# Decoder layer on one core: mixer weights split during the input projection, merge by chunks of 512 tokens

## The reference, cut to what matters

```
proj = h @ w_in                                  # (2048 x 1024) @ (1024 x 4864)
u, q, k, v, gate_pool, gate_att = split(proj)
pooled = einsum(multiscale_pool(u), w_pool_group)        # 512 channels
y_pool = (pooled * pool_scale) @ w_branch_pool           # 512 -> 1024
o = sum over 3 groups of softmax(lse) * group_output     # 256 channels
y_att = o @ w_branch_att                                 # 256 -> 1024
merged = sigmoid(gate_pool) * y_pool + sigmoid(gate_att) * y_att
y = merged @ w_out
x = x + gate * rmsnorm(y);  then a routed expert layer on x
```

## Time and profile before

| | |
|---|---|
| median of 3 runs | 2729.76 us (2728.51 to 2739.48) |
| the profiled execution: its time, its span | 2733.67 us, 2731.9 us |
| busy, share of the span | PE 87%, PEld 75%, DVE 49%, ACT 34%, POOL 20% |
| mean granted PE clock | 0.946 of full speed |
| merge | 1219 to 1415 us |
| mix_out, up to the start of its loop over tiles | 1415 to 1460 us |

### The profile page before, as it was taken

The page is one execution under the profiler, slowest core; times in us unless marked ns, Lnnn a source line. Parts: engine busy times, 40 slices in busy tenths (PEclk is TensorE's granted clock), DMA queues, the critical chain, the costliest instruction groups (busy, mean ns, idle before and its releaser), DMA issues. The chain is left out here.

```text
span 2731.9 us, 39222 instructions
## 1 busy us (share of the span) xinstructions
PE 2381.6 (87%) x13485; PEld 2039.5 (75%) x13486; DVE 1338.9 (49%) x1673; ACT 933.1 (34%) x1541; POOL 549.2 (20%) x375
## 2 busy tenths in 40 slices
PE   3599999999999968876969995699999999999990
PEld 3488888888888857764857884588898988988880
DVE  7552111123232257636534445888666384655536
ACT  3200000000000035533322221587666375655533
POOL 2311111111111020002334552222222222212220
PEclk9999999999999989957989996799999999999995
DMA  6123222223424233226555444599999597878847
GB/s 231 46 77 123 90 95 98 86 104 111 138 92 138 107 122 119 92 98 216 212 185 195 155 155 153 186 353 356 320 305 284 137 353 231 282 217 279 246 146 292
DMA packets 291435, 493.43 MB, mean 181 GB/s; under 512 B 21145, under 2 KB 226481, under 8 KB 281778
## 3 DMA queue, kind: packets, MB, share of 16 engines
q1 hardware_dynamic: 272658, 424.53, 44.9%
q0 software_dynamic: 14112, 51.39, 8.0%
q10 hardware_dynamic: 4608, 16.78, 1.5%
HBM read 374.98 MB, written 117.64 MB: 180 GB/s over the span
## 5 line engine op out<-in xcount | busy, mean ns | idle before, releaser
L357 PE MATMUL proj_psum<-h_hi,proj_w_hi 128*128 128x512 f32 x1216 | 481.7, 396 | 19.0 <-POOL proj_w_lo L342 19.0
L359 PE MATMUL proj_psum<-h_hi,proj_w_lo 128*128 128x512 f32 x1216 | 481.4, 396 | 0.0
L358 PE MATMUL proj_psum<-h_lo,proj_w_hi 128*128 128x512 f32 x1216 | 481.4, 396 | 0.0
L1585 PE MATMUL moe_p_gu<-moe_hi_gu,moe_xT_hi 128*128 128x256 f32 x1536 | 437.4, 285 | 1.7 <-DVE moe_xT_lo L1694 1.7
L378 DVE COPY proj_out<-proj_psum 128x512 f32<-128x512 f32 x152 | 123.7, 815 | 634.4 <-PE proj_psum L359 633.3
L1586 PE MATMUL moe_p_gu<-moe_lo_gu,moe_xT_hi 128*128 128x256 f32 x1536 | 428.7, 279 | 0.0
L1587 PE MATMUL moe_p_gu<-moe_hi_gu,moe_xT_lo 128*128 128x256 f32 x1536 | 428.6, 279 | 0.0
L1513 DVE TENSOR_TENSOR moe_lo_gu<-raw_gu,moe_hi_gu 128x1024 fp32r<-128x1024 f32 x256 | 302.1, 1220 | 23.5 <-ACT moe_hi_gu L1507 19.4
L335 ACT ACTIVATE proj_w_hi<-proj_raw 128x1024 fp32r<-128x1024 f32 x38 | 40.4, 1062 | 781.5 <-PE proj_psum L359 748.0
L1586 PEld LDWEIGHTS moe_p_gu<-moe_lo_gu,moe_xT_hi 128*128 128x128 f32 x1536 | 291.1, 190 | 2.1
L1585 PEld LDWEIGHTS moe_p_gu<-moe_hi_gu,moe_xT_hi 128*128 128x128 f32 x1536 | 289.2, 188 | 4.2 <-issue 2.1
(11 more groups left out here) (268 smaller groups left out, 3772.0 us busy)
## 6 DMA issues: line engine op xcount, KB each, us to landing
raw_gu<-in_w_exp_gate SPq DMA_DIRECT2D x256, 256.0 KB, 5.8
raw_gu<-in_w_exp_up SPq DMA_DIRECT2D x256, 256.0 KB, 5.9
raw_d<-in_w_exp_down SPq DMA_DIRECT2D x128, 512.0 KB, 7.9
projected<-proj_out SPq DMA_DIRECT2D x38, 1024.0 KB, 3.9
proj_raw<-in_w_in SPq DMA_DIRECT2D x38, 512.0 KB
att_qkv<-projected SPq DMA_DIRECT2D x18, 1024.0 KB
proj_w_rest<-in_w_ada SPq DMA_DIRECT2D x8, 2048.0 KB
merge_gate<-projected SPq DMA_DIRECT2D x32, 512.0 KB, 5.0
```

The source lines that it names most:

```text
L357: pe.matmul(bank, w_hi[:, u, k, :], h_hi[:, k, tok], start=(k == 0), stop=False)
L358: pe.matmul(bank, w_hi[:, u, k, :], h_lo[:, k, tok], start=False, stop=False)
L359: mm = pe.matmul(bank, w_lo[:, u, k, :], h_hi[:, k, tok], start=False, stop=(k == KD - 1))
L1585: pe.matmul(bank, x_hi, w_hi, start=first, stop=False)
```

## The change

Three edits.

1. **Weights.** While `project` runs its turns 1 to 10, SP also loads 128 x 512 pieces of the branch weights and of `w_out` (28 pieces, three a turn, ring of 4 in `w_rest`), ACT makes the hi part, POOL the lo part, and ACT stores both to DRAM (`branch_cut`, `out_cut`), a piece at a time: the next one waits for the stores of the one before. The loops of SP (first half), ACT, POOL and DVE in `project` are written out. `attend` loads the split branch weights on POOL (12 transfers of 512 KB, behind the bias of pairs 1 to 3) and, on SP, the group weights, the scale and the first 512 tokens of the pooled channels. `merge` loads six of the eight row blocks of the split `w_out` on POOL (12 transfers of 512 KB), one pair at m_ready 1, 3, 5, 7, 9 and 11; `mix_out` loads the other two (4 transfers of 512 KB) on POOL. No stage after `project` splits weights.
2. **Merge.** It goes by 4 chunks of 512 tokens. z, o and their lo parts have two chunk buffers. A step is one block of 128 channels by 512 tokens of one branch: 12 matmuls for the pooled branch, 6 for the attention branch, each into one of 4 banks in turn. First come the 8 pooled steps of chunk 0 while DVE combines the heads of chunk 0; then 24 steps of attention branch (chunk c) with pooled branch (chunk c + 1); then 8 of the attention branch alone. The pooled part of the next chunk is mixed and split inside a phase. The gates have rings of 11 (pooled) and 4 (attention) pieces of 128 x 512. The final addition goes from POOL to DVE, the store is 128 x 512, in place in the pooled gate's buffer.
3. **mix_out** waits for the split weights only at row blocks 6 and 7 of the first tile.

The diff, cut:

```diff
@@ project, SP
+                def load_later(n):
+                    if n >= CUT_RAW:
+                        sp.wait_ge(cut_lo_ready, n - CUT_RAW + 1)
+                    sp.dma_start(later_raw(n), later_rows(n)).then_inc(cut_loaded[n % CUT_RAW], 16)
...
-                with sp.Fori(1, FIRST_GATE) as j:
+                for j in range(1, FIRST_GATE):
                     pair_of_tiles(j)
+                    for n in later_of(j):
+                        load_later(n)
@@ project, ACT
-                with act.Fori(0, PAIRS) as j:
+                for j in range(PAIRS):
...
+                    for n in later_of(j):
+                        act.wait_ge(cut_loaded[n % CUT_RAW], 16 * (n // CUT_RAW + 1))
+                        if n:
+                            act.wait_ge(cut_stored, 32 * n)
+                        nc.scalar.activation(cut[:, 0, :].bitcast(F32R), later_raw(n), ACT.Copy).then_inc(cut_hi_ready, 1)
+                        act.wait_ge(cut_lo_ready, n + 1)
+                        for part in range(2):
+                            act.dma_start(later_cut(n, part), cut[:, part, :]).then_inc(cut_stored, 16)
@@ attend, SP and POOL
+                sp.dma_start(wg[:, :, :], w_pool_group[0].rearrange("g c d -> c g d")).then_inc(next_loaded, 16)
...
+                    if 1 <= q <= 3:
+                        for k in range(2 * q - 2, 2 * q):
+                            for part, w in enumerate((wb_hi, wb_lo)):
+                                pool.dma_start(w[:, k, :], branch_cut[part, ds(k * P, P), :]).then_inc(branch_loaded, 16)
@@ merge
+    CHUNK = 512
+    RP, RA, BANKS = 11, 4, 4
+        y_bank = lambda turn: psum[:, 4 + turn % BANKS, :]
+        def steps_of_stage():
+            for d in range(KD):
+                yield -KD + d, 0, d
+            for n in range(UNITS):
+                yield n, n // KD + 1, n % KD
@@ merge, SP
+                def load_p(n):
+                    d, tok = where(n)
+                    if n >= RP:
+                        sp.wait_ge(m_stored[n % RP], 16 * (n // RP))
+                    sp.dma_start(gate_p[:, n % RP, :], proj[ds((GATE_TILE + n % KD) * P, P), tok]).then_inc(p_loaded[n % RP], 16)
...
+                for n in range(UNITS):
+                    c, d = divmod(n, KD)
+                    if d == 0 and c + 2 < CHUNKS:
+                        load_pooled(c + 2)
+                    if n + RP - 1 < UNITS:
+                        load_p(n + RP - 1)
+                    if n + RA - 1 < UNITS:
+                        load_a(n + RA - 1)
+                    if d in (2, 4) and 2 * c + 3 + d // 2 < DUOS:
+                        load_heads(2 * c + 3 + d // 2)
+                    sp.wait_ge(m_ready, n + 1)
+                    sp.dma_start(merged[d_rows, tok], gate_p[:, n % RP, :]).then_inc(m_stored[n % RP], 16)
@@ merge, POOL
+                for k in range(EARLY_K):
+                    pool.wait_ge(m_ready, 2 * k + 1)
+                    for i, w in enumerate((wo_hi, wo_lo)):
+                        pool.dma_start(w[:, k, :], out_cut[i, ds(k * P, P), :]).then_inc(out_loaded, 16)
@@ merge, PE
+                mix_pooled(0, range(KP))
+                for n, phase, d in steps_of_stage():
+                    if n >= 0:
+                        if d == 0:
+                            pe.wait_ge(o_lo_ready, 2 * phase)
+                        branch(n, a_turn(n), KP, KP + KA, o_hi, o_lo)
+                    if phase < CHUNKS:
+                        if d == 0:
+                            pe.wait_ge(z_lo_ready, KP * (phase + 1))
+                        branch(n + KD, p_turn(n + KD), 0, KP, z_hi, z_lo)
+                        if d == 2:
+                            turn(2 * phase)
+                        if d == 4:
+                            turn(2 * phase + 1)
+                        if phase + 1 < CHUNKS and d in (5, 6):
+                            mix_pooled(phase + 1, range(2 * (d - 5), 2 * (d - 5) + 2))
@@ merge, DVE
+                def apply_a(n):
+                    dve.tensor_tensor(gate, y_bank(a_turn(n)), gate, ALU.mult).then_inc(y_taken, 1)
+                    dve.wait_ge(y_taken, a_turn(n) + 1)
+                    dve.tensor_tensor(gate_p[:, n % RP, :], gate_p[:, n % RP, :], gate, ALU.add).then_inc(m_ready, 1)
@@ mix_out
-                for k in range(KD):
-                    act.wait_ge(w_loaded[k % RAW], 16 * (k // RAW + 1))
-                    nc.scalar.activation(w_hi[:, k, :], w_raw[:, k % RAW, :], ACT.Copy).then_inc(w_hi_ready, 1)
+                for k in range(EARLY_K, KD):
+                    for i, w in enumerate((late_hi, late_lo)):
+                        pool.dma_start(w[:, k - EARLY_K, :], out_cut[i, ds(k * P, P), :]).then_inc(w_loaded[k - EARLY_K], 16)
...
+                        if k >= EARLY_K and t == 0:
+                            pe.wait_ge(w_loaded[k - EARLY_K], 32)
```

More of the change, by code:

```diff
@@ new lines, in merge @@
+        m_stored = [s.sem(f"m_stored{i}") for i in range(RP)]
+        (z_summed, z_hi_ready, z_lo_ready, steps, shifted, coef_exp, o_ready, o_turned, o_hi_ready, o_lo_ready, p_gated, a_gated,
+         y_summed, y_taken, m_ready, out_loaded) = (s.sem(n) for n in (
+             "z_summed", "z_hi_ready", "z_lo_ready", "steps", "shifted", "coef_exp", "o_ready", "o_turned", "o_hi_ready",
+             "o_lo_ready", "p_gated", "a_gated", "y_summed", "y_taken", "m_ready", "out_loaded"))
+        z_bank = lambda n: psum[:, n % 2, :]
@@ new lines, in load_a @@
+                def load_a(n):
+                    d, tok = where(n)
+                    if n >= RA:
+                        sp.wait_ge(m_ready, n - RA + 1)
+                    sp.dma_start(gate_a[:, n % RA, :], proj[ds((GATE_TILE + KD + n % KD) * P, P), tok]).then_inc(a_loaded[n % RA], 16)
+                load_heads(0)
+                load_p(0)
+                load_p(1)
+                load_heads(1)
+                for n in range(2, 6):
+                    load_p(n)
+                load_pooled(1)
@@ L828, in _ @@
-                high(DUOS // 2 - 1)
-                for n in range(UNITS):
-                    if n < KD:
-                        if n % 2 == 0:
-                            coefficients((KD + n) // 2)
-                        else:
-                            high((KD + n) // 2)
-                    act.wait_ge(gate_loaded[n % GATES], 32 * (n // GATES + 1))
-                    nc.scalar.activation(gate[:, n % GATES, :, :], gate[:, n % GATES, :, :], ACT.Sigmoid).then_inc(gated, 1)
-            @block.gpsimd
@@ new lines, in sigmoid_a @@
+                def sigmoid_a(n):
+                    act.wait_ge(a_loaded[n % RA], 16 * (n // RA + 1))
+                    nc.scalar.activation(gate_a[:, n % RA, :], gate_a[:, n % RA, :], ACT.Sigmoid).then_inc(a_gated, 1)
+                pooled_high(0, range(KP))
+                sigmoid_p(0)
+                for n, phase, d in steps_of_stage():
+                    if phase < CHUNKS:
+                        if d == 1:
+                            coefficients(2 * phase)
+                        if d == 3:
+                            high(2 * phase)
+                            coefficients(2 * phase + 1)
+                        if d == 5:
+                            high(2 * phase + 1)
+                        if phase + 1 < CHUNKS and d in (6, 7):
+                            pooled_high(phase + 1, range(2 * (d - 6), 2 * (d - 6) + 2))
+                    if -1 <= n < UNITS - 1:
+                        sigmoid_a(n + 1)
+                    if n + KD + 1 < UNITS:
+                        sigmoid_p(n + KD + 1)
@@ L939, in _ @@
[L939 to L953 removed]
+                    both = o[:, p % 2, :, :].rearrange("p i (h f) -> p i h f", h=HPG)
@@ new lines, in add_up, with apply_p @@
+                    chain.link(dve.tensor_tensor(both, hd[:, :, 0, :, 0:64], hd[:, :, 1, :, 0:64], ALU.add))
+                    dve.tensor_tensor(both, both, hd[:, :, 2, :, 0:64], ALU.add).then_inc(o_ready, 1)
+                def apply_p(n):
+                    gate = gate_p[:, n % RP, :]
+                    dve.wait_ge(p_gated, n + 1)
+                    dve.wait_ge(y_summed, p_turn(n) + 1)
+                    dve.tensor_tensor(gate, y_bank(p_turn(n)), gate, ALU.mult).then_inc(y_taken, 1)
@@ new lines, in _ @@
+                for n, phase, d in steps_of_stage():
+                    if phase < CHUNKS:
+                        if d == 1:
+                            add_up(2 * phase)
+                        if d == 3:
+                            low(2 * phase)
+                            add_up(2 * phase + 1)
+                        if d == 5:
+                            low(2 * phase + 1)
+                        if phase + 1 < CHUNKS and d in (6, 7):
+                            pooled_low(phase + 1, range(2 * (d - 6), 2 * (d - 6) + 2))
+                    if n >= 0:
+                        apply_a(n)
+                    if n + KD < UNITS:
+                        apply_p(n + KD)
@@ L1084, in low @@
```

(3 more changed lines are left out.)

357 lines of the change are left out of this document (154 added, 203 removed).

## The result

The changed kernel took 2718.24 us (median of 4 runs, 2715.77 to 2719.95), the kernel before 2731.82 us beside it (4 runs). The ratio is 0.9943, with a 95% interval of 0.9924 to 0.9961: faster by 13.6 us, where 36 were forecast. Of the profiled executions the span fell from 2731.9 to 2714.0 us.

What follows compares the result with a forecast made beforehand. PE was taken to bound project and merge from its first product, with closable gaps ahead of merge's products and at mix_out's start. Merge 24.5 plus mix_out 11.5 made 36 us off the 2729.8 median: 2694 us, range 2680 to 2717.

Steps and rivals of the forecast that it cites:

- The split in project: Project: extra loads, ACT copies, POOL subtractions and stores stay hidden behind PE, with 18.8 us of slack; cost 0 us.
- Merge's start: Merge before its first product: only four group matmuls remain, 9.2 us, first product at 1228.5 instead of 1275.1; gain 46.6 us.
- Merge's other work on PE: Merge: products 134.4 us, group matmuls 11.9, transposes 2.4, add_up wait 1.5, DVE-bound last steps 2, last addition 1.4.
- Merge's transfers: Merge, SP's loop: step of 3.9 us against PE's 4.8 in phases 1 and 2; loss 5 us, bounds 0 to 19.
- phase 1 runs at the DMA limit: Merge, phase 1: 13.2 MB in 38.4 us, 343 GB/s, against 354 or 338 with the engines full.
- mix_out's start: mix_out up to the row sums: DMA sets them at +24.5 instead of +36.0; gain 11.5 us, bounds 8 and 14.5.
- The stores hold SP: Merge: gate loads wait for the preceding step's store, 21 times; 2700 to 2715 chance 0.14, no change or slower 0.05.
- POOL and DVE did not block each other: Merge: rival that `w_out` issues on POOL stall DVE's additions, costing 10 us, 2704; chance 0.08.
- The split stayed hidden: Project: rival that the split does not stay hidden, 10 turns by 3 us, 2724; chance 0.06.
- PE over 95% busy in phases 1 to 3: Merge: sign that the forecast is right, PE busy over 95% in these phases.
- row sums near +25: mix_out: sign that the forecast is right, row sums about 25 us after the stage's start.
- PE waiting behind gates with SP waiting for `merged`: Merge: sign of wrong, PE waiting for y_taken behind DVE that waits for p_gated, with SP waiting for `merged`.

Runs made afterwards that it cites:

- the ring of 12: Changed kernel with 12 instead of 11 pooled-gate buffers, look-ahead still 10, so a load waits for the store before the newest: 2692.61 us; run again 2691.29.
- store first: Changed kernel with SP's step in merge issuing the store ahead of the next gate loads, ring and look-ahead unchanged: 2704.32 us, ratio 0.9897.
- one row block: Changed kernel with `EARLY_K = 1` instead of 6: one row block of `w_out` loaded in merge, seven in mix_out: 2734.93 us, ratio 1.0003.

## Why the prediction was wrong

The time is 24 us above the 2694 forecast and 1.2 us outside the range. That it came so near the range may be luck in part: in the profiled pair attend gave 7.2 us that no term of the forecast held. By its own steps:

- **The split in project at 0: right.** PE is busy 853.38 of 854 us (before: 852.86), although ACT's chain was slower than sized: it waited 62 us in 10 for stores of `out_cut` alone.
- **Merge's start, 46.6 us: right** (47.7). Three of the four group matmuls ran at the low clock, as taken (granted clock 0.50 up to 1218, 1.00 from 1220), and the four took 6.7 us, not 7.6.
- **Merge's other work on PE (134.4 + 11.9 + 2.4 + 1.5 + 2 + 1.4): right.** The sum without the 5 us for transfers has the last addition end 163.0 us after the stage's start. With SP's loop out of the way, in the two runs of the ring of 12, it ends 161.0 and 161.4 us after it.
- **Merge's transfers, 5 us with bounds 0 to 19: this is the step that failed.** It measured 29.7 us, the changed kernel's merge less that of the ring of 12 (27.9 against the forecast's own sum, 190.9 less 163.0). Its sentence was "With 2.7 us to landing, the time of a store twice as large, that is 3.9 us against PE's step of 4.8". The landing was read from stores that left with no load of SP's under way (13 of the 16) or with one, as SP's timeline of the kernel before shows for one of the latter:

```profile
1308.13 0.82 SPq L789 DMA_DIRECT2D merge_gate<-projected  x2
1312.81 0.33 SPq L802 DMA_DIRECT2D merged<-merge_gate  x1
1315.47 0.80 SPq L789 DMA_DIRECT2D merge_gate<-projected  x2
```

There the store left 3.9 us behind its loads; one of them had landed by then, at 1312.4, and the other landed at 1313.7. In the new order it leaves right behind them. It lands in 5.6 us (store first: 2.6), and the step is 6.54. The upper bound, the longest landing of before (4.6), was below the new median: a row taken under another order of issues was no bound at all. The upper bound of 19 did count all 21 steps; it was too low by the landing alone (and its 6 x 1.4 should be 6 x 1.6 by its own step of 5.9, 1 us).
- **The other half of that step, that phase 1 runs at the DMA limit, did not come about.** The two windows of merge move 213 and 204 GB/s at shares of 0.70 and 0.68; the wait kept the engines from filling. In the ring of 12, which asks for the bytes in time, the share from 1250 to 1345 is 0.86, and PE loses nothing by it (95.00 of 95 us): near the limit is not yet late. The rule cited there (the Trainium skill, DMA: Bandwidth & Descriptors, Queues, rings and completion order: an engine serves its queues in turn) gave 4 us for `w_out`; the runs give 11.3 for it. On a single store the 1.5 us by it come near the trace: 5.6 us with the stream, 4.5 with one row block of it. On merge the direction agrees and the size is off, since each delay of a store is passed on to the next load. The stream does not explain the other 18.4 us: the order of SP's own issues, with the wait for the newest store, does.
- **mix_out's start, 11.5 us: its size was off,** 14.5, the upper bound. Row sums at +21.5: PE ended the first tile there, and the transfers were not what came last. Its first product came at +8.0, where +8.5 was forecast. Not in the sum was the loop's loss of 2.8 us by the operands' place.
- **The rivals.** "The stores hold SP" is what happened, up to its formula: 21 steps x (6.54 - 4.8) - 6 = 30.5 us, where 29.7 were measured. With one row block in merge the formula gives 19.8 for 18.4, with the store first only 5.6 for 12.5, where the loads leave later and the lead of 6 is not there. The rival had 0.14 for 2700 to 2715 and 0.05 for no change; the result fell between the two. It was priced with landings of the earlier trace rows. POOL and DVE did not block each other: POOL issued a `w_out` load in 0.53 us, and DVE's additions stayed at 0.69. The split stayed hidden.
- **Signs.** PE over 95% busy in phases 1 to 3 and row sums near +25 did not show (5.3 of 42 us idle; +21.5). The one named for "wrong", PE waiting behind gates with SP waiting for `merged`, is what the profile shows, with ACT's copies of z and o as the link.

The sign of the change was right, and so was its main mechanism; one term took the gain back.

## What to carry to other kernels

When a transfer queue's step is load, load, store, and the next load waits for that store, the step is the store's landing behind the two loads, and it must fit in the step of the engine it feeds; price it with that order of issues, not with a landing read from another. Send the store ahead of the loads (2704 us here), or give the ring one more tile and let the load wait for the store before the newest (2692 us); don't spend that tile on more lead. Judge such a loop by its mean step, since the total of a wait also grows when the engine has nothing else to wait for.

## What the runs showed of the hardware

- A store of 256 KB that goes out right behind two gate loads of 256 KB on SP's queue landed in 5.6 us (median, 1250 to 1345), in 4.1 after the `w_out` stream had ended (1340 to 1385, 9 stores), and in 2.6 ahead of the loads with the `w_out` stream running. Issued from POOL it landed in 3.4. Ahead of the loads but with a step of 4.80 us instead of 5.35 it landed in 4.6. With no load of SP's under way it landed in 2.1 to 2.6 on SP's queue (store first, 11 stores) and in 2.4 to 3.1 on POOL's (9 stores). Twice the bytes in the kernel before: 2.7.
- In mix_out a 512-column matmul in float32r starts 227 ns after the one before it, or 233 ns where the early blocks of `w_out`, which stream through PE, begin 32 bytes past a multiple of 64 in each partition; two unused tiles of 32 bytes turn the one into the other. Project stays at 233 with both operands aligned, for a reason that no run here shows.
- A plain transfer of 512 KB costs POOL 0.53 us to issue, against up to 2.1 that were taken from its indirect ones.
- Attend, untouched among the changed kernel and those made from it, took 245.1 to 262.4 us with a mean granted clock of 0.88 to 0.79 of PE's full speed in it. That spread of 17 us is larger than the change's whole effect, and a single profile of before and after would have put it down to the change.
